# The MLP's down product by seven block products in place of eight, with the up product kept in DRAM

## What is computed

```
x = x + sq_relu_ffn(rms_norm(x, norm_ffn_g[i]), w_ffn1[i], w_ffn2[i])

def sq_relu_ffn(h, w1, w2):
    return jnp.square(jax.nn.relu(h @ w1)) @ w2
```

## Time and profile before

| | |
|---|---|
| runs (us) | 2593.98 median; 2592.67, 2593.98, 2595.39 |
| profiled execution, first to last instruction | 2593.0 us (the page gives no other time of its own for it) |
| busy, share of the span | PE 98%, PEld 93%, DVE 46%, POOL 42%, ACT 23% |
| chain that ended last | PE 91%, of it line 247 alone 80% of the span |
| DMA | 134 MB, mean 52 GB/s |

### The profile page before, as it was taken

How to read it: one execution, slowest core, us unless ns; L and a number is a source line. 1 busy time by engine, 2 the same in 40 slices (tenths; PEclk the granted TensorE clock), 3 DMA queues, 4 the chain that set the end, 5 groups by cost and what they waited for, 6 DMA issues and landing times.

```text
span 2593.0 us, 38698 instructions
## 1 busy us (share of the span) xinstructions
PE 2533.6 (98%) x16459; PEld 2402.8 (93%) x16459; DVE 1195.4 (46%) x1596; ACT 600.5 (23%) x892; POOL 1083.1 (42%) x899
## 2 busy tenths in 40 slices
PE   8999999999999999999999999989999999999998
PEld 7999866999999999999978997679999999999998
DVE  4333389443333323333468888753433333433324
ACT  4200277221101011010238823641201101101010
POOL 4423256334443344433442424945344433444331
PEclk9999999999999999999999998999999999999999
DMA  6111210211111111111041111011111111111111
GB/s 219 34 49 35 84 49 2 84 49 50 49 33 48 49 49 48 33 49 49 21 145 33 34 50 54 2 75 43 49 49 49 32 49 49 49 49 32 49 33 67
DMA packets 93117, 134.17 MB, mean 52 GB/s; under 512 B 13214, under 2 KB 78838, under 8 KB 92503
## 3 DMA queue, kind: packets, MB, share of 16 engines
q1 hardware_dynamic: 90374, 115.40, 13.9%
q10 hardware_dynamic: 2640, 17.31, 1.7%
HBM read 113.16 MB, written 18.73 MB: 51 GB/s over the span
## 4 chain that ended last, share of the span: by engine, by line
PE 91%; DVE 5%; POOL 1%; ACT 1%; issue 1%; DMA 0%; SPq 0%; DVEq 0%; ACTq 0%
PE PS L247 80%; PE PS L906 1%; PE PS L967 1%; PE PS L1316 1%; PE PS L944 1%; PE PS L1345 1%; PE PS L1285 1%; POOL Lb L1680 1%; PE PS L589 1%; DVE Z L1581 0%; DVE score L1478 0%; PE PS L911 0%; POOL yc L1667 0%; PE PS L1167 0%; PE PS L613 0%
## 5 line engine op out<-in xcount | busy, mean ns | idle before, releaser
L1871 POOL TENSOR_TENSOR w_sp<-stage,ones 128x512 fp32r<-128x512 f32 x372 | 382.0, 1058 | 1342.9 <-PE PS L247 1287.0
L247 PE MATMUL PS<-h,w_sp 128*128 128x352 f32 (+1 forms) x5184 | 857.4, 325 | 13.1 <-DVE h L535 6.6
L247 PEld LDWEIGHTS PS<-h,w_sp 128*128 128x128 f32 (+1 forms) x5184 | 839.7, 188 | 20.0 <-issue 15.1
L247 PE MATMUL PS<-hid,w_sp 128*128 128x352 f32 x4608 | 749.0, 323 | 0.0
L247 PEld LDWEIGHTS PS<-hid,w_sp 128*128 128x128 f32 x4608 | 744.7, 188 | 0.0
L247 PE MATMUL PS<-hz,w_sp 128*128 128x352 f32 x3456 | 567.7, 323 | 0.0
L247 PEld LDWEIGHTS PS<-hz,w_sp 128*128 128x128 f32 x3456 | 558.7, 188 | 0.0
L1875 POOL TENSOR_TENSOR w_sp<-stage,w_sp 128x512 fp32r<-128x512 f32 x372 | 524.3, 1439 | 0.0
L338 DVE TENSOR_TENSOR xT<-PS,xT 128x1056 f32<-128x1056 f32 x248 | 311.4, 1256 | 345.7 <-PE PS L247 345.7
L304 ACT ACTIVATE rbuf<-rbuf 128x1056 f32<-128x1056 f32 x64 | 69.6, 1088 | 1234.3 <-DVE rbuf L328 1234.3
L328 DVE SCALAR_TENSOR_TENSOR rbuf<-PS,rstd 128x1056 f32<-128x1056 f32 x64 | 80.4, 1257 | 505.4 <-PE PS L247 505.4
(11 more groups left out here) (286 smaller groups left out, 1563.6 us busy)
## 6 DMA issues: line engine op xcount, KB each, us to landing
stage<-in_w_ffn SPq DMA_DIRECT2D x64, 1024.0 KB, 5.3
stage<-in_w_in_even SPq DMA_DIRECT2D x10, 1024.0 KB, 5.0
stage<-in_w_in_odd SPq DMA_DIRECT2D x9, 1024.0 KB, 5.1
x_spill<-xT ACTq DMA_DIRECT2D x2, 4224.0 KB, 13.1
xT<-x_spill ACTq DMA_DIRECT2D x2, 4224.0 KB, 12.5
xtok<-in_x_prompt SPq DMA_DIRECT2D x8, 512.0 KB, 8.9
stage<-in_w_out_even SPq DMA_DIRECT2D x4, 1024.0 KB, 9.2
stage<-in_w_out_odd SPq DMA_DIRECT2D x4, 1024.0 KB, 5.0
```

What stands on the lines that cost most here:

```text
L247: mm = pe.matmul(out[0:m, c, :], lhs, rhs(k, b)[:, c * CH:(c + 1) * CH], start=(i == 0 and n == 0), stop=(i == nk - 1 and n == 2))
L1871: pool.tensor_tensor(w_sp[:, s, 0, q:q + 512], stage[:, s, q:q + 512], ones[:, 0:1].to_broadcast([P, 512]), ALU.mult).then_inc(w_hi_done, 1)
```

## The change

The down product is cut into 2x2 blocks: the 1,024 output features into two halves of 512, the hidden features of a chunk into two halves, the tokens into two halves of 528. Strassen's scheme (Winograd's form, with 7 products and sums of blocks before and after) replaces the 8 block products. Per layer:

- The up product runs first as a whole: 16 units, 32 jobs. DVE forms four sums of half-width hidden blocks per unit (`combine`), and SP stores eight blocks (2.16 MB) to DRAM.
- The down product then runs in 8 chunks of 512 hidden features. Per chunk SP loads 2 MB of weights into the two stage buffers and seven pairs of hidden blocks (0.54 MB each) from DRAM. POOL forms 8 weight sums and 14 low parts of 512 columns (`split_down`), ACT 14 high parts of the weights (`w_high`) and 7 of the hidden blocks (`b_high`), DVE the 7 low parts of the hidden blocks (`b_low`).
- A tile of the down product is 128 x 528: 2 contraction blocks x 3 passes x 2 matmuls of 264 columns; 28 tiles per chunk (7 products x 4), each in one of four pairs of banks. DVE adds a tile into `xT` or into one of three accumulators (`aux`); in the last chunk DVE and POOL (`combine_last`) combine these into `xT`.
- The next weights may be loaded only after POOL's last low part of this chunk (`down_weights` waits for `wl_done`), since the sums are made in place in the stage buffers.
- `dve_n2`/`act_n2` are rewritten to run between the last tiles of layer 0, and the first unit of the odd projection is split by POOL ahead of `combine_last`.

The matmuls of the down product go from 2,304 of 352 columns to 2,688 of 264 per layer. Its core (names of line numbers below are those of the changed kernel):

```diff
-                for m in range(KT):
-                    gemm_tile(pe, j + m, u % 2, 2, m * P, D, P, lambda k, b: hid[:, c % 2, k, b, :], dj2)
+        def down_tile(pe, L, t, q, m, dt=0):
+            pe.wait_ge(pt_free, PT_L * L + t - 3 + dt) if PT_L * L + t >= 4 else None
+            out = pair_banks(L, t)
+            for i in range(2):
+                for n, (a, b) in enumerate(((0, 0), (0, 1), (1, 0))):
+                    for c in range(2):
+                        mm = pe.matmul(out[:, c, :], w2[q][i][:, a, m * P:(m + 1) * P],
+                                       Bq[q][:, b, i, c * QN:(c + 1) * QN], start=(i == 0 and n == 0),
+                                       stop=(i == 1 and n == 2))
+            mm.then_inc(pt_done, 1)
...
+            def prepare(c, d=0, first=False):
+                for q in range(7):
+                    act.wait_ge(pt_done, PT_L * L + 28 * (c - 1) + 4 * q + 4 + d * 28)
+                    if q == 0 and not first:
+                        b_high(c - 1, 6, d)
+                    w_high(c, q, d)
+                    if q:
+                        b_high(c, q - 1, d)
...
+            def combine(i, d=0):
+                x = ob[i % 2]
+                n = 4 * (16 * L + i)
+                dve.wait_ge(s_done, 2 * (16 * L + i) + 2 + d * 2)
+                dve.tensor_tensor(x[:, 4, :], x[:, 1, :], x[:, 0, :], ALU.subtract).then_inc(t_done, 1)
+                dve.tensor_tensor(x[:, 6, :], x[:, 3, :], x[:, 1, :], ALU.subtract).then_inc(t_done, 1)
+                dve.wait_ge(t_done, n + 1 + d * 4)
+                dve.tensor_tensor(x[:, 5, :], x[:, 3, :], x[:, 4, :], ALU.subtract).then_inc(t_done, 1)
+                dve.wait_ge(t_done, n + 3 + d * 4)
+                dve.tensor_tensor(x[:, 7, :], x[:, 2, :], x[:, 5, :], ALU.subtract).then_inc(t_done, 1)
...
+            def b_low(n, d=0):
+                q = n % 7
+                n += 7 * NCHK * L
+                dve.wait_ge(bh_done, n + 1 + d * 7)
+                dve.tensor_tensor(Bq[q][:, 1, :, :], B_raw[q][:, :, :], Bq[q][:, 0, :, :].bitcast(F32),
+                                  ALU.subtract).then_inc(bl_done, 1)
...
+            def down(t, q, m, d=0, first=False):
+                dve.wait_ge(pt_done, PT_L * L + t + 1 + d * 28)
+                x, src = halves(target(q, m)), pair_banks(L, t)
+                if first and q not in TARGET:
+                    ins = dve.tensor_copy(x, src)
+                else:
+                    ins = dve.tensor_tensor(x, src, x, ALU.add)
+                ins.then_inc(pt_free, 1)
...
+            for q in range(7):
+                for m in range(4):
+                    down(4 * q + m, q, m, first=True)
+                    if q == 0 and m == 1:
+                        combine(15)
+                for n in ((2,), (3, 4), (5, 6), (), (7, 8), (9, 10), (11,))[q]:
+                    b_low(n)
+            with dve.Fori(0, 6) as i:
+                for q in range(7):
+                    for m in range(4):
+                        down(28 + 4 * q + m, q, m, i)
+                    b_low(7 + q + 5, i)
...
+            def last(m, before=()):
+                t0 = 196 + 7 * m
+                own = PT_L * L + t0
+                a1, a5, a6 = (aux[:, m, x, :] for x in range(3))
+                x11, x12, x21, x22 = (xT[:, k + m, n:n + HN] for k in (0, 4) for n in (0, HN))
+                down(t0, 0, m)
+                down(t0 + 1, 1, m)
+                down(t0 + 2, 2, m)
+                down(t0 + 3, 3, m)
+                if m == 0:
+                    b_low(55)
+                dve.wait_ge(pt_free, own + 4)
+                ch.link(dve.tensor_tensor(a6, a6, a1, ALU.add))
+                down(t0 + 4, 4, m)
+                dve.wait_ge(pt_free, own + 5)
+                dve.tensor_tensor(x22, x22, a6, ALU.add).then_inc(cb_u, 1)
+                dve.wait_ge(cb_u, 4 * L + m + 1)
+                dve.tensor_tensor(x21, x21, x22, ALU.add).then_inc(cb_x, 1)
+                dve.wait_ge(cb_x, 4 * L + m + 1)
+                down(t0 + 5, 5, m)
+                dve.wait_ge(cb, 16 * L + 4 * m + 4)
+                down(t0 + 6, 6, m)
...
+            def between(m):
+                if m == 1:
+                    square(1)
+                if m == 2:
+                    square(2)
+                    square(3)
+                    square(4)
+                    low(2)
+                if m == 3:
+                    low(6)
+                    low(0)
+                    low(4)
+                    low(5)
+                    low(1)
+                    square(5)
+                    low(3)
+                    low(7)
+                    square(6)
+                    square(7)
...
+                def down_weights(k, d=0):
+                    K, i = NCHK * L + k // 2, k % 2
+                    if k < 2:
+                        sp_.wait_ge(w_split, u0 + 15 + k)
+                    else:
+                        sp_.wait_ge(wl_done, 14 * (K - 1) + 13 + i + d * 14)
+                    src = wd[:, bass.ds(d * 4 + 2 * k, 2), :] if k >= 4 else wd[:, 2 * k:2 * k + 2, :]
+                    sp_.dma_start(stage_dn[(u0 + k) % 2], src).then_inc(v_stage[i], 16)
...
+                def chunk(c, d=0):
+                    down_weights(2 * c, d)
+                    down_weights(2 * c + 1, d)
+                    for q in range(7):
+                        sp_.wait_ge(pt_done, PT_L * L + 28 * (c - 1) + 4 * q + 4 + d * 28)
+                        hidden(c, q, d)
...
+            def split_down(c, L, u0, d=0):
+                K = NCHK * L + c
+                st = [stage[:, (u0 + i) % 2, :] for i in range(2)]
+                for q in range(7):
+                    for i in range(2):
+                        a11, a21, a12, a22 = (st[i][:, 512 * x:512 * x + 512] for x in range(4))
+                        if q == 2:
+                            if c == 0 and i == 0:
+                                evacuated(pool, (J_F0, J_F1)[L] + 30)
+                                evacuated(pool, (J_F0, J_F1)[L] + 31)
+                            pool.wait_ge(v_stage[i], 16 * (K + 1) + d * 16)
+                            ins = pool.tensor_tensor(Sx[i][:, :], a21, a22, ALU.add)
+                        elif q == 3:
+                            ins = pool.tensor_tensor(Sx[i][:, :], Sx[i][:, :], a11, ALU.subtract)
+                        elif q == 4:
+                            ins = pool.tensor_tensor(a21, a11, a21, ALU.subtract)
+                        elif q == 6:
+                            ins = pool.tensor_tensor(Sx[i][:, :], a12, Sx[i][:, :], ALU.subtract)
+                        if q in S_AT:
+                            ins.then_inc(s_rdy, 1)
+                    for i in range(2):
+                        a11, a21, a12, a22 = (st[i][:, 512 * x:512 * x + 512] for x in range(4))
+                        x = {0: a11, 1: a12, 4: a21, 5: a22}.get(q, Sx[i][:, :])
+                        pool.wait_ge(wh_done, 14 * K + 2 * q + i + 1 + d * 14)
+                        pool.tensor_tensor(w2[q][i][:, 1, :], x, w2[q][i][:, 0, :].bitcast(F32),
+                                           ALU.subtract).then_inc(wl_done, 1)
...
+            def combine_last(L):
+                for m in range(4):
+                    t = PT_L * L + 196 + 7 * m
+                    a1, a5, a6 = (aux[:, m, x, :] for x in range(3))
+                    x11, x12, x21, x22 = (xT[:, k + m, n:n + HN] for k in (0, 4) for n in (0, HN))
+                    pool.wait_ge(pt_free, t + 3)
+                    pool.tensor_tensor(x11, x11, a1, ALU.add).then_inc(cb, 1)
+                    pool.tensor_tensor(x12, x12, a5, ALU.add).then_inc(cb, 1)
+                    pool.wait_ge(cb_u, 4 * L + m + 1)
+                    pool.wait_ge(cb, 16 * L + 4 * m + 2)
+                    pool.tensor_tensor(x12, x12, a6, ALU.add).then_inc(cb, 1)
+                    pool.wait_ge(cb_x, 4 * L + m + 1)
+                    pool.tensor_tensor(x22, x22, a5, ALU.add).then_inc(cb, 1)
...
+            down_all(0, U_F0)
             split(U_OIN)
+            combine_last(0)
```

More of the change, by code:

```diff
@@ L69 @@
 J_F1 = J_OOUT + 8
-NCHUNK = FF // 256
+NPAIRS = FF // 256
+NCHK = 8
+HN = NT // 2
+QN = HN // 2
+PT_L = 28 * NCHK
+BLK = [0, 2, 4, 5, 6, 7, 3]
+S_AT = {2: 0, 3: 1, 4: 2, 6: 3}
 TOPK = 256
@@ L285, in pe_ffn, with pair_banks @@
-            with pe.Fori(0, 7) as i:
[L286 to L291, removed]
+            with pe.Fori(0, 7) as i:
+                for t in (1, 2):
+                    gemm_in_unit(pe, u0 + t, j0 + 2 * t, du=i * 2, dj2=i * 2, rhs=ffn_h)
+            gemm_in_unit(pe, u0 + 15, j0 + 30, rhs=ffn_h)
+        def pair_banks(L, t):
+            b = 2 * ((0, 3, 1, 2), (2, 3, 1, 0))[L][t % 4]
+            return PS[:, b:b + 2, 0:QN]
@@ new lines, in pe_down, with operands @@
+        def pe_down(pe, L, j0):
+            evacuated(pe, j0 + 30)
+            def operands(c, q, d=0):
+                pe.wait_ge(wl_done, 14 * (NCHK * L + c) + 2 * q + 2 + d * 14)
```

(54 more changed lines are left out.)

308 lines of the change are left out of this document (181 added, 127 removed).

## The result

| | before | changed |
|---|---|---|
| median of the runs (us) | 2593.42 (4 runs) | 2572.76 (4 runs, 2571.92 to 2575.32) |
| ratio, 95% interval | | 0.992 (0.9906 to 0.9935) |
| span of the profiled execution | 2593.0 | 2570.2 |

Faster by 0.8%, where no change was forecast (2598). The wide range (2566 to 2638) held the time; the sign and the forecast's own range (2584 to 2612) did not. The page after, which answers to the earlier trace rows: PE has lost two hundredths of its share, and DVE and POOL are now over half busy.

The account below looks back on a forecast made before the run. PE's matmuls were taken to bound the MLPs, every new wait paid in full. -73.6 + 46 + 21 + 4 + 7 = +4.4 us against 2593.0 gave 2598 us, no change; own range 2584 to 2612, wide range 2566 to 2638.

Parts of the forecast that it names:

- product at its pace: Down product, both layers: 2,688 matmuls at 124.4 ns replace 2,304 at 161.1 per layer, saving 73.6 us.
- chunk 0, both layers: First down chunk: PE waits for POOL, ACT and DVE before chunk 1, 23 us a layer, +46.
- end of layer 0: Last chunk and seam: PE waits 11 us for final sums, 5 for the norm, 5 before the next projection, +21.
- end of layer 1: Some 2 us in the last chunk and 2 more before the output's transposes, +4.
- clock: After PE waits of over 3.3 us, slow-clock stretches: four at 1.7 us, +7.
- the 14.4 ns: Old MLP matmuls of 352 columns: the part of 161.1 ns that is not streaming; taken as paid per matmul.
- rival 1: Down product: matmul shorter than taken (120.8 ns if non-streaming time grows with columns, or less), 2581 us; chance 0.25.
- Covered: Up and down products: stores, loads and DVE's differences (3 us per unit) stay hidden, costed at nothing.
- Rivals 2 and 3: Down matmuls: streaming and weight load collide, 130 to 135 ns, 2624 to 2648 us, chance 0.22; the other is rival 3.
- rival 3: Waits are smaller: chunk 0 waits 12 us, not 23, giving 2576 us; chance 0.08.

Follow-up runs that it names:

- e1: Kernel before, with other matmul widths in the looped MLP chunks: 231.4 ns a matmul at 512 columns, 121.4 at 264, 111 at 220 and at 176.
- e5: Kernel before, other widths, some weights of 64 columns: 111.7 ns at 176 columns with 128 weight columns, 83 with 64; 59.9 at 128 columns with 64.
- e2: Changed kernel, POOL's eight weight sums of chunk 0 cut from 512 to 8 columns, products 2, 3 and 6 reading an unsummed block: 2560.15 us (one run).
- e6: Changed kernel, ACT's high parts of the weights three products later and the next weights' load behind the loads of four pairs: 2574.14 us, ratio to before 0.9922.
- e3: Changed kernel, DVE's low parts of chunk 1's pairs moved back by one product: 2569.04 us, ratio to before 0.9907.
- e4: Changed kernel, POOL's final sums of layer 0 put ahead of the split of the odd projection's first unit: 2581.01 us, ratio 0.9949.
- e7: Changed kernel, last chunk's products 0 to 3 run for all four row groups before products 4 to 6 group by group: 2576.48 us, ratio 0.993.
- e8: Changed kernel with e6 and e7 together, three groups of POOL's final sums ahead of the split, its high parts on ACT: 2548.78 us, ratio to before 0.9827.

## Why the prediction was wrong

| term (us) | forecast | measured | from |
|---|---|---|---|
| product at its pace | -73.6 | -90.2 | 2 x 2,688 x 121.3 against 2 x 371.2 |
| chunk 0, both layers | +46 | +42.6 | 62.69 and 61.41, less 40.76 each |
| end of layer 0 | +21 | +16.4 | last chunk 57.52 less 40.76, 2.9 of seam, less 3.3 that stand under clock |
| end of layer 1 | +4 | +3.9 | last chunk 42.50 less 40.76, idle before the transposes 3.6 for 1.4 |
| clock | +7 | +8.1 | chunk 1 43.30 and 43.09 less 40.76 each; 1.6 twice in layer 0's last chunk |
| elsewhere | 0 | -3.6 | mostly the up products, 374.6 a layer where 747.1 less 371.2 left 375.9 |
| sum | +4.4 | -22.8 | 2570.2 - 2593.0 |

- **The step that failed** is "if the 14.4 ns are paid per matmul, 110.0 + 14.4 = 124.4 ... I take 124.4, since each matmul still loads its own 128 weight columns". The term was mis-sized by 16.6 us of the 27 that the forecast missed; with 121.3 in its place the same sum would have been -12.2, faster. In e1 and e5 the part paid per matmul is small: at 264, 352 and 512 columns a matmul costs 4.3 + 0.4435 a column, and what the weights cost beside that shows only as a floor (111 to 112 ns) at 220 and below. The 14.4 ns at 352 columns are 11.3 at 264 (121.3 less 110.0), so they came down most of the way to the 10.8 of growth with the columns, which was the second value named in the same sentence (120.8) and rival 1.
- **Rival 1** named this mechanism, at 2581; the time came 8 us below it, since the other terms came out smaller in sum. Its steady chunks were to be 1.2 us shorter or more; they are 1.0 shorter (40.76 for 41.8), and PE has no idle in them, so POOL's floor lies below that.
- **Chunk 0** was right in mechanism, link by link: POOL, ACT's high part, DVE; and in its end, 62.7 for 65. The weights landed 34.7 and 38.6 after the start, where 37.5 and 40 were forecast. It was wrong in the place of the idle: some 23 us were forecast before the first tile of chunk 1, and 4.2 are there (4.4 in layer 1). 10.7 (9.3) stand before product 6, because the low parts of chunk 1's pairs 0 and 1 already stand ahead of product 5's evacuations. The end does not depend on that, since the chain up to pair 3 sets it. e2 and e6 show that POOL's work and when it may begin set a large part of the wait; e3, that DVE's order mostly places it.
- **The end of layer 0** was right in mechanism and somewhat large: the first final sum behind the split, at the eleventh tile as forecast, 10 us of idle for 11, 3.5 for 5, 2.9 of seam for 5. e4 and e7 show the dependence: whichever of the two comes second, PE waits for it.
- **The clock** was right in its count: four stretches at 0.50 lie on PE's path, 8.1 us for 7. Into chunk 1 they cost 2.5 and 2.3 us. In layer 0's last chunk they cost 1.6 each (180 matmuls took 23.64 us and 36 took 6.15, 0.2 of each the last record's own tail, where 21.8 and 4.4 would do). The stretch after the idle of 10.66 us, in product 6 (48 matmuls in 7.68 us for 5.8), delayed nothing, since DVE came to these tiles only at 989.72. The transposes after layer 1 ran at 0.50 at first too (10.63 us for 8.06 in the earlier trace rows); that cost nothing, since from their start to the end of the span it is 16.3 us, where it was 17.0. Two stretches of the changed kernel, columns as above:

```profile
978.60:982.20 3.60, 3.59 (x16) 3.60 (x17) 2.02 (x4) 2.24 (x3) 3.60 (x4) 0.50 0.00 0
990.50:995.90 5.40, 5.40 (x25) 5.40 (x25) 4.64 (x5) 0.84 (x2) 5.40 (x5) 0.50 0.01 3
```

- **Covered**: right. The stores are free and the steady chunks have no idle PE at 145 GB/s. DVE's four differences took 6.2 us a unit (1.2 to 1.8 each by the mean of their lines), not 3, and cost PE nothing.
- **The rule of the Trainium skill** ("TensorE: Matmul & The Clock Gate", "Back-to-back issue gap": N/2.4 + 2.5) gives 112.5 ns at 264; the trace has 121.3, e1 231.4 at 512 where the rule has 215.8. The section gives this rule for an isolated matmul, and says that in a stream of weight loads and matmuls both set the spacing; so it was no forecast for this kernel, and the prediction left that condition out. Against the line measured here its fixed part is near (2.5 for 4.3) and its slope is 6% low.
- **Rivals 2 and 3** fell: 121.3 is no collision, and chunk 0 waits 22 and 21, not 12. That rival 3's time (2576) came nearest to the measured one is luck.

## What to carry to other kernels

One width gives no law: where a change alters the shape of a matmul, a second width of the same type in any trace (or one run that measures it) decides between a price per matmul and a price per column. Here this one term missed by more (16.6 us) than all the waits together. Making matmuls narrower pays only down to the width at which the floor begins, here some 242 columns for 128 weight columns (an estimate from e1 and e5); by the same figures a matmul of 132 columns would take an estimated 112 ns, where the line alone gives 63. A wait that comes from an engine's shortage of time mostly moves when one order is changed (e3, e4, e6, e7); in the one run where much of it went (e8), the place to which it moved had other work to run.

## What the runs showed of the hardware

- The pace of fp32r matmuls with their own weights at granted clock 1.00 rises by 0.4435 ns a column between 264 and 512 columns (e1), above the 0.4167 that one column a cycle at 2.4 GHz would be.
- With 88 columns and weights of 128 the clock of e5 fell to 0.50 though the rows show PE busy throughout, and matmuls took 14.0/68 = 206 ns, 1.8 times the floor; the up jobs between them came back to 1.00. Before it fell PE ran matmuls of 128 columns with 64 weight columns at 1.00. Stretches of e5:

```profile
1683.00:1687.00 4.00, 4.00 (x71) 4.00 (x69) 1.39 (x2) 2.17 (x2) 3.15 (x3) 1.00 0.02 4
...
1700.00:1714.00 14.00, 14.00 (x68) 14.00 (x67) 4.31 (x4) 0.00 (x0) 0.00 (x0) 0.50 0.21 68
```

- A weight transfer of 1 MB landed in 8.0 us (median) during the changed kernel's up products, beside the stores of the hidden blocks, and in 5.6 to 5.8 during its down products, beside the loads of the pairs; before it was 5.3. Neither shows in PE's pace in the up products or the steady chunks.
